# Choice of experts: query projections behind the sub-keys, three places with 512 columns, dense steps moved to the first two heads

## The reference

```python
PEER_HEADS, PEER_N_KEYS, PEER_QDIM, PEER_TOPK, PEER_BLOCK = 8, 128, 256, 16, 128

def peer_ffn(h, w_q, sub_keys, u_tab, v_tab):
    def one_block(hb):
        q = (hb @ w_q).reshape(PEER_BLOCK, PEER_HEADS, 2, PEER_HALF)
        sc = jnp.einsum('thcd,hcnd->thcn', q, sub_keys).astype(jnp.float32)
        s1, i1 = lax.top_k(sc[:, :, 0], PEER_TOPK)
        s2, i2 = lax.top_k(sc[:, :, 1], PEER_TOPK)
        cand_s = (s1[..., :, None] + s2[..., None, :]).reshape(...)
        cand_i = (i1[..., :, None] * PEER_N_KEYS + i2[..., None, :]).reshape(...)
        top_s, pos = lax.top_k(cand_s, PEER_TOPK)
        idx = jnp.take_along_axis(cand_i, pos, axis=-1)
        g = jax.nn.softmax(top_s, axis=-1)
        act = jax.nn.gelu(jnp.einsum('thkd,td->thk', u_tab[idx], hb))
        wts = (g * act.astype(jnp.float32)).astype(hb.dtype)
        return jnp.einsum('thk,thkd->td', wts, v_tab[idx])
```

## Time and profile before

| | |
|---|---|
| time, median of 3 runs | 2954.53 us (2951.0 to 2954.92) |
| the profiled execution: its own time, and its span | 2953.12 us, 2951.3 us |
| granted TensorE clock, mean | 0.997 |
| PE busy | 2908.2 us (99%), 13947 matmul records |
| DVE, ACT, POOL busy | 1907.9 (65%), 1152.7 (39%), 841.3 us (29%) |
| chain of waits that ended last | PE 84%, DVE 12%, ACT 3%, issue 1% |

### The profile page before, as it was taken

The page is one execution under the profiler, slowest core; times in us unless marked ns, Lnnn a source line. Parts: engine busy times, 40 slices in busy tenths (PEclk is TensorE's granted clock), DMA queues, the critical chain, the costliest instruction groups (busy, mean ns, idle before and its releaser), DMA issues.

```text
span 2951.3 us, 35553 instructions
## 1 busy us (share of the span) xinstructions
PE 2908.2 (99%) x13947; PEld 2494.6 (85%) x13947; DVE 1907.9 (65%) x3257; ACT 1152.7 (39%) x1704; POOL 841.3 (29%) x521
## 2 busy tenths in 40 slices
PE   8999999999999999999999999999999999899999
PEld 6877777889889899998999999998888877688887
DVE  6664666679888894436878788875444567654443
ACT  5674565433333334423323223323222356532221
POOL 0000000227888888872332233321000300200000
PEclk9999999999999999999999999999999999999999
DMA  4325554436666667798988888842322321133222
GB/s 145 110 90 215 200 216 176 139 108 141 130 128 155 143 156 150 165 279 318 337 308 308 285 309 317 315 149 89 100 93 93 118 85 52 51 98 100 93 94 71
DMA packets 240807, 489.28 MB, mean 166 GB/s; under 512 B 97664, under 2 KB 149440, under 8 KB 240128
## 3 DMA queue, kind: packets, MB, share of 16 engines
q1 hardware_dynamic: 175680, 417.87, 43.0%
q0 software_dynamic: 64960, 69.14, 10.2%
HBM read 443.18 MB, written 77.23 MB: 176 GB/s over the span
## 4 chain that ended last, share of the span: by engine, by line
PE 84%; DVE 12%; ACT 3%; issue 1%; DMA 0%; SPq 0%; ACTq 0%
PE pb L717 27%; PE pb L719 26%; PE pb L718 26%; DVE whl L1753 2%; ACT scr L1274 1%; PE pb L1012 1%; DVE ST L1753 1%; DVE su L2005 1%; DVE ST L1761 1%; DVE ST L2006 1%; DVE S L1753 1%; DVE su L2008 1%; ACT whl L1277 1%; PE pb L895 1%; DVE sm L2007 1%
## 5 line engine op out<-in xcount | busy, mean ns | idle before, releaser
L717 PE MATMUL pb<-H,whl 128*128 128x512 f32 (+1 forms) x2400 | 940.0, 392 | 5.6 <-DVE H L1753 2.0
L719 PE MATMUL pb<-H,whl 128*128 128x512 f32 (+1 forms) x2400 | 912.0, 380 | 0.0
L718 PE MATMUL pb<-H,whl 128*128 128x512 f32 (+1 forms) x2400 | 911.3, 380 | 0.0
L1753 DVE TENSOR_TENSOR whl<-raw,whl 128x1024 fp32r<-128x1024 f32 (+5 forms) x554 | 651.7, 1191 | 248.7 <-ACT whl L1277 247.4
L1277 ACT ACTIVATE whl<-raw 128x1024 fp32r<-128x1024 f32 (+5 forms) x554 | 544.7, 1003 | 358.7 <-PE pb L719 357.6
L717 PE MATMUL pb<-S,whl 128*128 128x448 f32 (+2 forms) x1732 | 653.3, 377 | 7.4 <-DVE whl L1753 3.0
L719 PE MATMUL pb<-S,whl 128*128 128x448 f32 (+2 forms) x1732 | 648.5, 374 | 0.0
L718 PE MATMUL pb<-S,whl 128*128 128x448 f32 (+2 forms) x1732 | 648.5, 374 | 0.0
L717 PEld LDWEIGHTS pb<-H,whl 128*128 128x128 f32 x2400 | 451.3, 188 | 83.0 <-issue 8.7
L718 PEld LDWEIGHTS pb<-H,whl 128*128 128x128 f32 x2400 | 451.4, 188 | 72.6 <-issue 6.0
L719 PEld LDWEIGHTS pb<-H,whl 128*128 128x128 f32 x2400 | 450.6, 188 | 73.0
(11 more groups left out here) (226 smaller groups left out, 2513.2 us busy)
## 6 DMA issues: line engine op xcount, KB each, us to landing
raw<-in_pu SPq DMA_DIRECT2D x128, 512.0 KB, 4.4
raw<-in_pv SPq DMA_DIRECT2D x128, 512.0 KB, 6.3
raw<-in_w_in SPq DMA_DIRECT2D x72, 512.0 KB, 4.0
ad<-scr SPq DMA_DIRECT2D x128, 224.0 KB, 4.5
GA<-gd SPq DMA_DIRECT2D x60, 448.0 KB, 4.1
GA<-ad SPq DMA_DIRECT2D x60, 448.0 KB, 5.3
raw<-in_wg SPq DMA_DIRECT2D x44, 512.0 KB, 3.7
raw<-in_wu SPq DMA_DIRECT2D x44, 512.0 KB, 4.2
```

Source lines behind the costliest of these rows:

```text
L717: e.matmul(o, lh, h, start=start, stop=False, skip_group_check=True)
L718: e.matmul(o, lh, l, start=False, stop=False, skip_group_check=True)
L719: return e.matmul(o, ll, h, start=False, stop=stop, skip_group_check=True)
L1753: return e.tensor_tensor(o, x, y, op)
```

## The change

It only changes the order of the list that `peer_order` writes and the width of twelve dense steps. The list of weight units follows from it, so loads and conversions move along.
- `pq(1, 0)` stands right behind the sub-keys of head 0. From there on `pq(h + 1, 1)` follows `sk(h + 1, 0)`, and `pq(h + 2, 0)` follows `sk(h + 1, 1)`. `lo(h + 1, 1)` now stands between `cand` and `best`, eight dense steps behind its projection.
- Sixteen more dense steps stand in head 0 (between `cand` and `best`, and behind sk(1, 1)), and eight more ahead of `cand` in head 1, 24 in all. So share(0) of the last blocks, which stood behind u[80:88], stands behind u[96:104], and share(1), which stood behind u[144:152], stands behind u[168:176]. From head 2 to the end of the choice each step has 24 more dense steps ahead of it, and the stretch between the last `store` and the dot products is that much shorter.
- Twelve dense steps are made with all 512 columns: four behind sk(7, 1), four at store(0, 0) and four at store(1, 0). What lies in the last 64 columns of the bank is not read.

```diff
-    out, s = [], 0
-
-    def u(n):
+    out, whole, s = [], set(), 0
+
+    def u(n, wide=0):
         nonlocal s
+        whole.update(range(s, s + wide))
         for _ in range(min(n, 1024 - s)):
             out.append(("u", s))
             s += 1
@@
     out.append(("sk", 0, 0))
     out.append(("sk", 0, 1))
+    out.append(("pq", 1, 0))
@@
     for h in range(8):
         bs = (0 if h else 2, 4)
         for c in range(2):
-            if h < 7:
-                out.append(("pq", h + 1, c))
             out.append(("top", h, c, bs))
-            if h < 7:
-                out.append(("lo", h + 1, c))
-            u((8 + 8 * c if h < 7 else 16) if h else 8)
+            if h < 7 and c == 0:
+                out.append(("lo", h + 1, 0))
+            u((8 + 8 * c + 8 * (h == 1) * c if h < 7 else 16) if h else 8)
         for c, step in enumerate(("cand", "best")):
             out.append((step, h, bs))
             if h < 7:
                 out.append(("sk", h + 1, c))
-            u((16 if h < 7 and c == 0 else 8) if h else 8 * c)
+                if h + c < 7:
+                    out.append(("pq", h + 1 + c, 1 - c))
+                if c == 0:
+                    u(8)
+                    out.append(("lo", h + 1, 1))
+            u(8, 4 if h == 6 and c else 0)
@@
-                u(8)
+                u(8, 0 if part else 4)
@@
-                        linear(ju, bank[i % 2], Hdh, Hdl, h2, ("u", i), (k,), n=TD)
+                        if step[1] in whole:
+                            linear(ju, bank[i % 2], Hh, Hl, h2, ("u", i), (k,))
+                        else:
+                            linear(ju, bank[i % 2], Hdh, Hdl, h2, ("u", i), (k,), n=TD)
```

More of the change, by code:

```diff
@@ L71, in unit_order @@
     u += [("w_out", m, 1024) for m in range(8)]
-    for step in peer_order():
+    for step in peer_order()[0]:
         if step[0] == "pq":
@@ L290, in peer_order @@
     u(1024)
-    return out
+    return out, whole
 IN2 = (0, 1, 2, 3, 10, 11)
@@ L678, in build @@
         attention = attention_order()
-        choice = peer_order()
+        choice, whole = peer_order()
         mixing, mixbank = mixer_order()
```

## The result

The changed kernel takes **2966.9 us** (median of 5 runs, 2964.69 to 2969.56); beside it the kernel before took 2954.53 us (5 runs, 2951.0 to 2955.51). The ratio is 1.0046, 95% interval 1.0035 to 1.0057: slower by 10 to 17 us. The forecast was 2968, slower.

What follows compares the result with a forecast made beforehand. TensorE, busy 99%, was taken as the bound, with GpSimd's adds a second chain that never catches up. Stands of +15.7 us less 0.9 gained gave +14.8 on the profiled 2953.12: 2968 us, range 2963 to 2974 (78%), 2961 to 2976 with half-rivals.

Steps and rivals of the forecast that it cites:

- The second chain: GpSimd's adds to the table: start when share(1) is done, end 564 us later whatever the others do, 2.02 us an add.
- Share(1) late by 16.6 us: Shares of the second head, behind 24 more dense steps and pq(3,0): ready at 756.8 us instead of 740.26, last add equally late.
- GpSimd's wait ahead of the second head: Sign in the profile after: GpSimd's wait ahead of the second head's adds near 25 us instead of 8.6.
- TensorE's stands: At u[936:944] and the unit before, TensorE waits for low halves held up by late rows: some 18 us in all.
- The clock term: Half clock behind the long stand, in the two units before u952: costs 1.7 us.
- Pace and small stands: Dense steps behind projections: some 72 groups at 4.86 instead of 4.96 us, -7.2 us; six stands gone, -2.4; second projection's weights, +2.6.
- 512 columns: 36 matmuls at three places cost 22 ns more each, +0.8 us; the skill's columns-only rule would give 1.0 us and no pace.
- (2): Rival, partly hidden: adds get quicker during stands or rows 0 to 3 land sooner; 3 to 8 us remain, 2959 us; 6%.
- (4): Rival: pace stays slow behind 12 wide matmuls or a projection; only 0.9 us, 2969 us; forecast including it has 78%.
- (5): Rival: waits for the second projection's weights grow to 1.5 us a head; swallowed unless (1) holds, then 2952 us; no separate chance.
- (1): Rival: GpSimd's adds hold nothing up, so the pace terms stand alone: -6.2 us, 2947 us; chance 8%.
- (3): Rival: late gathers run beside denser traffic, land after 11 us, and bring more half clock: +23 us, 2977 us; chance 8%.

Runs made afterwards that it cites:

- before_dots_later: Kernel before with 12 instead of 14 rows of the first table under the dense steps, so each dot stands 16 dense steps later; ratio 0.9994.
- steps_only: Kernel before with only the dense steps moved, 16 more in one head and 8 in the next, ahead of share(1); 2961.37 us against 2953.51, ratio 1.0028.
- wide_only: Kernel before with only the 512 columns at the three places, in the old order; 2954.14 us against 2954.07, ratio 1.0001.
- late_start_only: Kernel before with GpSimd's adds of the second head also waiting for the end of projection pq(3,1); 2967.1 us against 2957.31, ratio 1.0041.
- after_8_fewer_adds: Changed kernel without 8 of the 40 adds of the last head; 2954.9 us against 2957.31 for the kernel before, ratio 0.9995.
- first_projection_dots_wide: Kernel before with only first projections moved behind the sub-keys, dots 16 dense steps later, 512 columns at three places; 2948.01 us against 2957.31, ratio 0.9968.
- before_fewer_adds: Kernel before without 16 of the 40 adds of the last head; 2958.97 us against 2953.51, ratio 1.0019.
- after_fewer_adds: Changed kernel without 16 of the 40 adds of the last head; 2956.1 us, ratio 1.0010 against the kernel before.
- third_head_on: Kernel before with both projections' new places from the third head on, eight dense steps brought forward, 448 columns everywhere; 2953.39 us against 2953.51, ratio 0.9997.

## Why the prediction was right

It was right in direction, size (2968 against 2966.9 us) and mechanism. By its steps:

- **The second chain.** Shown. 2.017 us an add before, 2.016 in the changed kernel; where the start moved by 11.9 us or more with all adds kept, the end moved with it to within 2.1 us. The spacing is less fixed than I had it, though: 1.98 to 2.03 us over the kernels with all adds. In before_dots_later, with no edit to the adds or what feeds them, the chain was 4.1 us longer, in the two versions with only the first projection moved 7 to 11 us shorter. The prediction's "whatever the others do" is too strong, and the traces hint at who has a hand in it: in the kernel before the median add takes 1.86 us, and 62 of the 279 spacings are over 2.05 us. For 60 of the 62 most of what VectorE does meanwhile are the operations TENSOR_TENSOR and TENSOR_SCALAR (conversions, and the arithmetic of the picks), while of 66 adds beside its searches (MAX8, FIND_INDEX8) none is that long. No run tested it.
- **Share(1) late by 16.6 us.** Measured (the 1.74 us are those lost before the change begins) 758.80 - 740.54 - 1.74 = 16.5 us. The sum of VectorE's steps behind pq(3, 0) held. Such a sum from the real predecessor is what served: the simpler count by TensorE's steps alone, which I used for steps_only, was 3 us too large, since VectorE had been behind TensorE and caught up. One sign named was off: GpSimd's wait ahead of the second head is 18.7 us, not 25, because the first head's adds end later too (737.84 against 730.35 us), which changes nothing behind it.
- **TensorE's stands.** Some 18 us and 1.7 us of half clock were forecast; 4.05 + 11.13 = 15.2 us of stands and 3.3 us of half clock came: unit 116 took 17.79 - 11.13 = 6.7 us and units 117 and 118 11.23 us, where 4.86 and 9.73 are usual. The sum is nearly the same, 18.5 against 19.7. The clock term was undersized, since two stands, not one, were followed by half clock; the stand was oversized, by 1.5 us since row 1 was there that much sooner (gather 3.9 us behind the last add, not 4.9), and by the 1.8 us of half clock in unit 116, which TensorE would have stood for row 1 otherwise. So the first half clock cost nothing, and the 1.5 us of row 1 make up what the forecast had too much: 13.3 us came at the second table where 14.8 were forecast.
- **Pace and small stands.** Up to unit 111 the terms gave -4.5 us (the forecast of -6.2 less the 17 groups from unit 111 on); measured -3.7. Two terms were mis-sized. The wait for the second projection's weights was put at 0.5 us in five heads: from start to start the five places took 0.41, 0.79, 0.79, 0.71 and 0.79 us instead of 0.11, and their projections 5.57 to 5.60 us where 5.54 is usual: 3.1 us, not 2.6. And the six small stands that go were worth 0.32 us each (a unit with the sub-keys and the stand took 6.47 us, without the stand 6.15), 1.9 us, not 2.4. The pace itself, 4.86 for 4.96 us, came as read the earlier trace rows.
- **512 columns.** The rule from the Trainium skill (page "TensorE: Matmul & The Clock Gate", section "Back-to-back issue gap"), by which the isolated gap follows from the columns alone, leaves no room for a second pace: the units behind a wide place would have stayed at the 4.96 us that they had. The trace does not agree: 4.87 us in wide_only, with nothing else changed. The measurement decides.
- **Behind it.** The second table starts 15.1 us later on the clock of the profile (1388.01 - 1372.94), 13.3 us when both are counted from the same matmul; 1388 was forecast. The span of the profiled execution is 16.4 us longer: 1.7 of them were lost before the change begins, 1.3 behind the start of the second table, where the two kernels do the same. Against the medians, 12.4 us, the forecast of 14.8 is 2.4 us too high, within the interval of 10 to 17. That 2968 lies 1.1 us from the measured 2966.9 is in part luck: the sum was set on a profiled execution 1.4 us under the median of before. One sum of the range is off by 1 us: the low end of the forecast is 2967.9 - 1.7 - 1 - 1.2 = 2964, not 2963.
- **Rivals.** (2), partly hidden, and (4), no pace, did not come; (5) came in a small part, as said. (1), the adds hold nothing up, would be 2947 us: late_start_only excludes it for the kernel before, after_8_fewer_adds for the changed one. What it says of the pace was right in kind, though: the two versions in which the adds hold nothing up are some 5 and 9.5 us faster than before by their ratios. (3), a collision of the late chain, did not come in the changed kernel; what looks like one, of other transfers, came where the chain ended *earlier*, which none of my cases had.

## What to carry to other kernels

An engine that never waits for long and that nobody waits for may still be a chain with its own length. Find what starts it and what comes behind its last instruction, take the slack there, and check every moved step against it: here 24 dense steps that cost TensorE nothing, and one projection, shifted the start of 280 adds by 16 us past a slack of 1.5 us. The cheapest cure was on the consumer's side (later dots), and of a reordering with two parts the half that asked nothing of another engine kept the gain (unit 111 came 4.0 us earlier with it and later dots, 3.7 us with the whole change).

## What the runs showed that I had not expected

- **Ending the adds sooner made the kernel slower**: 16 adds less cost the kernel before 0.19% (0.10 to 0.28), 5.5 us by the medians. The one trace has a stand of 2.45 us on TensorE and a store that landed so late that ScalarE waited 10.24 us for it; two reads of 1.8 MB stand 4.6 us apart there instead of 25.7. That is some 2 of the 5.5 us; the rest is open.
- **The pace of equal matmuls has a memory**: in every trace of these kernels 448 columns go at 202.7 ns from start to start behind any place with 512 (but for the four units of wide_only named above), and mostly at 206.7 behind products with 128, for as long as nothing else comes between (units 105 to 126 of first_projection_dots_wide, all at 4.86 to 4.87 us). A stand can change it either way: behind its 2.45 us before_fewer_adds went from 4.96 to 4.86 us a unit, behind its 4.53 us after_fewer_adds from 4.86 to 4.96. What in the engine holds this was not tested; nor did the prediction need it, which took the two paces from rows.
- **A stand can be paid twice**: behind waits of 4.05 and 11.13 us the granted clock was 0.56 and 0.50 over some 3 us, and the units behind them took 1.8 and 1.5 us more. Only the second counted, since behind the first TensorE would have waited for a row anyway. Behind the wait of 1.62 us in third_head_on the next unit took 4.94 us, so nothing was lost.
